# Gates and branch products of the second block: 512 weight columns move instead of 256 token columns

## The reference

```python
z = h @ w_in                              # gz: its last 4 * 1024 columns
branches = (gmlp, pool, sparse_attention, conv)   # four tensors, 256 tokens x 256 features
gates = sigmoid(gz.reshape(B, S, 4, 1024))
y = gates[:, :, 0] * (branches[0] @ w_branch[0])
for n in range(1, 4):
    y = y + gates[:, :, n] * (branches[n] @ w_branch[n])
return y @ w_out
```

## Time and profile before

| | |
|---|---|
| median of three runs | 1937.95 us |
| profiled execution | 1937.7 us |
| its span (first to last instruction) | 1936.0 us |
| PE busy | 1923.7 us, 99% |
| DVE busy | 1380.9 us, 71% |
| ACT busy | 928.1 us, 48% |
| POOL busy | 237.5 us, 12% |

### The profile page before, as it was taken

The page is one execution under the profiler, slowest core; times in us unless marked ns, Lnnn a source line. Parts: engine busy times, 40 slices in busy tenths (PEclk is TensorE's granted clock), DMA queues, the critical chain, the costliest instruction groups (busy, mean ns, idle before and its releaser), DMA issues.

```text
span 1936.0 us, 29945 instructions
## 1 busy us (share of the span) xinstructions
PE 1923.7 (99%) x11950; PEld 1723.8 (89%) x11950; DVE 1380.9 (71%) x1588; ACT 928.1 (48%) x1032; POOL 237.5 (12%) x195
## 2 busy tenths in 40 slices
PE   9999999999999999999999999999999999999998
PEld 7999888889998888888899998888888899998887
DVE  7777766668677666766769677667766769677666
ACT  6564444346545344544554445444544554446443
POOL 0000000000001000000049250000000049250000
PEclk9999999999999999999999999999999999999999
DMA  7544555554356555555444555555555454555553
GB/s 280 193 153 174 176 196 194 184 187 172 131 199 210 190 193 174 193 190 192 163 175 153 175 194 193 183 191 181 202 192 189 167 177 153 173 191 179 188 193 109
DMA packets 50738, 353.37 MB, mean 183 GB/s; under 512 B 6064, under 2 KB 6192, under 8 KB 9040
## 3 DMA queue, kind: packets, MB, share of 16 engines
q1 hardware_dynamic: 47952, 341.93, 50.6%
q0 software_dynamic: 2400, 9.99, 1.5%
q10 hardware_dynamic: 288, 0.05, 0.0%
HBM read 349.85 MB, written 2.10 MB: 182 GB/s over the span
## 4 chain that ended last, share of the span: by engine, by line
PE 90%; DVE 7%; ACT 2%; issue 1%; DMA 0%; DVEq 0%; POOL 0%; POOLq 0%; SPq 0%; ACTq 0%
PE ps L225 21%; PE ps L190 18%; PE ps L191 18%; PE ps L192 18%; PE ps L227 11%; DVE w_lo L166 2%; DVE conv_y L2123 1%; ACT w_hi L159 1%; DVE score L2171 1%; PE ps L1286 1%; ACT a L1667 0%; DVE top L2166 0%; PE ps L2304 0%; DVE score L2143 0%; DVE a L395 0%
## 5 line engine op out<-in xcount | busy, mean ns | idle before, releaser
L166 DVE TENSOR_TENSOR w_lo<-raw,w_hi 128x2048 fp32r<-128x2048 f32 x317 | 734.6, 2321 | 279.8 <-ACT w_hi L159 278.8
L159 ACT ACTIVATE w_hi<-raw 128x2048 fp32r<-128x2048 f32 x317 | 606.3, 1915 | 402.4 <-PE ps L192 226.1
L225 PE MATMUL ps<-a,w_hi 128*128 128x512 f32 x1792 | 449.7, 392 | 2.6 <-DVE w_lo L166 1.4
L225 PEld LDWEIGHTS ps<-a,w_hi 128*128 128x128 f32 x1792 | 325.6, 189 | 67.2 <-DVE a L395 2.8
L190 PE MATMUL ps<-mixH,w_hi 128*128 128x256 f32 x1168 | 334.4, 286 | 0.3
L191 PE MATMUL ps<-mixL,w_hi 128*128 128x256 f32 x1168 | 330.4, 283 | 0.0
L192 PE MATMUL ps<-mixH,w_lo 128*128 128x256 f32 x1168 | 330.3, 283 | 0.0
L190 PE MATMUL ps<-w_hi,mixH 128*128 128x512 f32 x736 | 287.7, 391 | 0.0
L191 PE MATMUL ps<-w_lo,mixH 128*128 128x512 f32 x736 | 287.2, 390 | 0.0
L192 PE MATMUL ps<-w_hi,mixL 128*128 128x512 f32 x736 | 286.4, 389 | 0.0
L227 PEld LDWEIGHTS ps<-a,w_lo 128*128 128x128 f32 x1792 | 244.4, 190 | 17.5
(11 more groups left out here) (382 smaller groups left out, 2035.6 us busy)
## 6 DMA issues: line engine op xcount, KB each, us to landing
raw<-in_w_b SPq DMA_DIRECT2D x198, 1024.0 KB, 5.0
raw<-in_w_a SPq DMA_DIRECT2D x124, 1024.0 KB, 4.8
rows<-in_post_gains POOLq DMA_DIRECT2D x6, 512.0 KB, 4.3
rows<-in_rows_a POOLq DMA_DIRECT2D x2, 1028.0 KB, 7.1
raw<-in_w_a SPq DMA_DIRECT2D x4, 512.0 KB, 6.9
x<-in_x SPq DMA_DIRECT2D x2, 512.0 KB, 5.5
bias_line<-a_gates POOLq DMA_DIRECT2D x1, 1024.0 KB, 4.8
out<-x SPq DMA_DIRECT2D x4, 256.0 KB, 2.0
```

The source lines that it names most:

```text
L159: act.activation(k.w_hi[:, s, :], k.raw[:, s, :], ACT.Copy).then_inc(k.hi_ready, 1)
L166: dve.tensor_tensor(k.w_lo[:, s, :], k.raw[:, s, :], k.w_hi[:, s, :].bitcast(F32), ALU.subtract).then_inc(k.lo_ready, 1)
L225: pe.matmul(both, hi[:, kt, cols], k.a[:, :, kt, :], start=kt == 0, stop=False)
```

## The change

- **Gates**: chunk 9+2g and chunk 10+2g now hold 512 gate columns together, the first with k-tiles 0 to 3, the second with 4 to 7. `gate(i)` calls `t_chunk` with 512 columns: activations stationary, 24 matmuls of 512 weight columns in a chunk. The result lies token by feature in two banks (one for each tile of 128 tokens), banks 6 and 7 for even pairs, 0 and 1 for odd ones, accumulated over two chunks. ACT makes the tanh after every second chunk, two of 512 columns.
- **Branch products**: chunk 25+i holds 512 output columns (half h = i//2) of two branches (q = i%2). It is computed first for token tile 0, then for tile 1, 24 matmuls of 512 columns. DVE multiplies tile 0 by its gates as soon as that half of the chunk is done (`branch_tile`), tile 1 after the chunk.
- **The sum over the branches** of a half of the features is complete only after two chunks. POOL writes it to `mixed[h][tt]`, and in half 1 DVE may overwrite the products only after POOL's last addition of half 0 (`mix_ready`).
- **Transposes**: PE transposes `mixed` back to feature by token, eight transposes for each half (`mixed_transpose`), half 0 between the products 27 and 28, half 1 between the output chunks 29 and 30. ACT and DVE then split the transposed sum out of PSUM.
- Other small tiles move to other PSUM banks, and the weights are packed on the host to match.

```diff
-                for i in range(4):
-                    g = gated[i % 2]
-                    for n in (0, 2):
-                        pool.wait_ge(branch_ready.sem, branch_ready.at(l, NBR * i + n + 2))
-                        pool.tensor_tensor(g[n], g[n], g[n + 1], ALU.add).then_inc(ch.sem, ch.one())
-                    pool.wait_ge(ch.sem, ch.at(l))
-                    pool.tensor_tensor(g[0], g[0], g[2], ALU.add).then_inc(mix_ready.sem, 1)
+                for h in range(2):
+                    for tt in range(TT):
+                        g = gated[tt]
+                        pool.wait_ge(branch_ready.sem, branch_ready.at(l, NBR * 2 * h + 2 * tt + 2))
+                        pool.tensor_tensor(g[0], g[0], g[1], ALU.add).then_inc(ch.sem, ch.one())
+                    for tt in range(TT):
+                        g = gated[tt]
+                        pool.wait_ge(branch_ready.sem, branch_ready.at(l, NBR * (2 * h + 1) + 2 * tt + 2))
+                        pool.tensor_tensor(g[2], g[2], g[3], ALU.add).then_inc(ch.sem, ch.one())
+                        pool.wait_ge(ch.sem, ch.at(l))
+                        pool.tensor_tensor(mixed[h][tt], g[0], g[2], ALU.add).then_inc(mix_ready.sem, 1)
...
                 def gate_in(i):
-                    act.wait_ge(k.chunk_done, st.results(l, G0 + i))
-                    act.activation(flat(gates[:, 2 * i:2 * i + 2, :]), k.ps[:, (i + 1) % 2, :], ACT.Tanh, scale=0.5)\
-                       .then_inc(f_evicted.sem, 1)
+                    if i % 2 == 1:
+                        g = i // 2
+                        for tt in range(TT):
+                            if tt == 0:
+                                act.wait_ge(gate_tile.sem, gate_tile.at(l, g + 1))
+                            else:
+                                act.wait_ge(k.chunk_done, st.results(l, G0 + i))
+                            act.activation(gates_t[:, tt, g // 2, g % 2, :], k.ps[:, (6, 0)[g % 2] + tt, :], ACT.Tanh, scale=0.5)\
+                               .then_inc(gate_evicted.sem, 1)
                     high.upto(G0 + i + 3)
...
-                for i in range(4):
-                    high.upto(min(BR + 3 + i, F0[1] - 1))
-                    act.wait_ge(mix_ready.sem, mix_ready.at(l, i + 1))
-                    act.activation(flat(nH[:, 2 * i:2 * i + 2, :]), gated[i % 2][0], ACT.Copy, scale=0.5)\
-                       .then_inc(mixH_ready.sem, 1)
+                for h in range(2):
+                    high.upto((BR + 4, BR + 6)[h])
+                    for b in range(2):
+                        i = 2 * h + b
+                        act.wait_ge(mixT_done.sem, mixT_done.at(l, i + 1))
+                        act.activation(flat(nH[:, 2 * i:2 * i + 2, :]), k.ps[:, mixed_banks[h][b], :], ACT.Copy, scale=0.5)\
+                           .then_inc(mixH_ready.sem, 1)
...
+                def gate_branches(i):
+                    h, q = i // 2, i % 2
+                    for tt in range(TT):
+                        if tt == 0:
+                            dve.wait_ge(branch_tile.sem, branch_tile.at(l, i + 1))
+                        else:
+                            dve.wait_ge(k.chunk_done, st.results(l, BR + i))
+                        if h == 1:
+                            dve.wait_ge(mix_ready.sem, mix_ready.at(l, tt + 1))
+                        for n in range(2):
+                            dve.scalar_tensor_tensor(gated[tt][2 * q + n], gates_t[:, tt, 2 * q + n, h, :], 1.0,
+                                                     k.ps[:, 4 * ((i + 1) % 2) + 2 * n + tt, :], ALU.add, ALU.mult)\
+                               .then_inc(branch_ready.sem, 1)
+
+                for i in range(3):
                     low.upto(BR + 2 + i)
...
+                    gate_branches(i)
+                mix_low(0)
+                gate_branches(3)
                 low.upto(BR + 6)
-                mix_low(3)
+                mix_low(1)
...
+                def branch(i):
+
+                    s, q = (BR + i) % SLOTS, i % 2
...
+                    pe.wait_ge(k.lo_ready, st.count(l, BR + i))
+                    for tt in range(TT):
+                        for n in range(2):
+                            for kk in (2 * n, 2 * n + 1):
+                                a = [v[:, tt * P:(tt + 1) * P] for v in aop(4 * q + kk)]
+                                ins = product(pe, k.ps[:, 4 * ((i + 1) % 2) + 2 * n + tt, :], a, (hi[:, kk, :], lo[:, kk, :]),
+                                              kk == 2 * n, kk == 2 * n + 1)
+                        ins.then_inc(branch_tile.sem if tt == 0 else k.chunk_done, 1)
+
+                def mixed_transpose(h):
+
+                    pe.wait_ge(mix_ready.sem, mix_ready.at(l, 2 * h + 2))
+                    for b, bank in enumerate(mixed_banks[h]):
+                        for kk in range(2):
+                            for tt in range(TT):
+                                ins = pe.transpose(k.ps[:, bank, kk * SEQ + tt * P:kk * SEQ + (tt + 1) * P],
+                                                   mixed[h][tt][:, (2 * b + kk) * P:(2 * b + kk + 1) * P], k.ident)
+                        ins.then_inc(mixT_done.sem, 1)
...
+                branch(1)
+                pe.wait_ge(branch_ready.sem, branch_ready.at(l, NBR))
+                branch(2)
+                pe.wait_ge(branch_ready.sem, branch_ready.at(l, NBR * 2 + 2))
+                mixed_transpose(0)
+                branch(3)
                 pe.wait_ge(branch_ready.sem, branch_ready.at(l, NBR * 3))
+                pe.wait_ge(mix_split.sem, mix_split.at(l, 2))
...
                     t_chunk(k, pe, WO + i, range(2 * i, 2 * i + 2), DM, nop, t_out, i == 0, False)
+                    if i == 0:
+                        pe.wait_ge(branch_ready.sem, branch_ready.at(l, NBR * 4))
+                        mixed_transpose(1)
```

More of the change, by code:

```diff
@@ L1409, in second_block @@
                  [GU[:, n * 512:(n + 1) * 512] for n in range(3)] + [yb2[:, :, :].rearrange("p t n -> p (t n)")]]
+        gates_t = gates[:, :, :].rearrange("p (t n h a) m -> p t n h (a m)", t=TT, n=NBR, h=2)
         pz = sb("pz", [P, 2, POOL_PAD + SEQ])
@@ L1416, in second_block @@
         conv_y = sb("conv_y", [P, 2, SEQ])
+        mixed = [[qkF[:, 2 * tt:2 * tt + 2, :].rearrange("p f n -> p (f n)") for tt in range(TT)],
+                 [v[:, :, :].rearrange("p f n -> p (f n)") for v in (idxF, conv_y)]]
+        mixed_banks = ((4, 6), (0, 1))
         conv_p = sum4[:, :, 0:SEQ]
@@ L1880, in _ @@
                     half = slice(e * 64, (e + 1) * 64)
-                    ins = act.activation(yH[half, 2 + j, :], k.ps[half, 4 + 2 * e, j * SEQ:(j + 1) * SEQ], ACT.Copy,
+                    ins = act.activation(yH[half, 2 + j, :], k.ps[half, 4 - e, j * SEQ:(j + 1) * SEQ], ACT.Copy,
                                          scale=par[half, PB_PS + j:PB_PS + j + 1])
@@ new lines, in mix_low @@
+                def mix_low(h):
+                    for b in range(2):
+                        i = 2 * h + b
+                        dve.wait_ge(mixH_ready.sem, mixH_ready.at(l, i + 1))
+                        dve.scalar_tensor_tensor(flat(nL[:, 2 * i:2 * i + 2, :]), k.ps[:, mixed_banks[h][b], :], 0.5,
+                                                 flat(nH[:, 2 * i:2 * i + 2, :]).bitcast(F32), ALU.mult, ALU.subtract)\
+                           .then_inc(mix_split.sem, 1)
+                def gate_branches(i):
[11 more added lines that the diff above has]
+                               .then_inc(branch_ready.sem, 1)
@@ L2490, in _, with gate @@
                 feature(6)
+                def gate(i):
+                    g, half = (i - 9) // 2, (i - 9) % 2
+                    pe.wait_ge(k.lo_ready, st.count(l, M0 + i))
+                    if half == 0 and g == 0:
+                        pe.wait_ge(rel_ready.sem, rel_ready.at(l, 1))
+                    elif half == 0 and g == 1:
+                        pe.wait_ge(f_evicted.sem, f_evicted.at(l, 6))
+                    elif half == 0:
+                        pe.wait_ge(gate_evicted.sem, gate_evicted.at(l, 2 * (g - 1)))
+                    t_chunk(k, pe, M0 + i, range(4 * half, 4 * half + 4), 512, nop,
+                            lambda tt, h: k.ps[:, (6, 0)[g % 2] + tt, :], half == 0, half == 1,
+                            tile_done=gate_tile.sem if half == 1 else None)
                 def to_features(bank, src, by=None):
@@ L2515, in _ @@
                 feature(8)
-                feature(9)
+                gate(9)
                 def scores(qt):
@@ L2529, in _ @@
                 scores(1)
-                feature(10)
+                gate(10)
                 pe.wait_ge(rel_ready.sem, rel_ready.at(l, 1))
@@ L2533, in _ @@
                 for i in range(11, 17):
-                    feature(i)
+                    gate(i)
                 pe.wait_ge(exp_ready.sem, exp_ready.at(l, 2))
@@ L2542, in _ @@
                 ins.then_inc(pT_done.sem, 1)
-                feature(17)
```

(17 more changed lines are left out.)

63 lines of the change are left out of this document (20 added, 43 removed).

## The result

The changed kernel takes 1949.70 us (median of four runs, 1949.27 to 1951.04), the kernel before beside it 1937.99 (four runs). The ratio is 1.0061, 95% interval [1.0050, 1.0073]: slower by 11.7 us, where +8.6 to +8.8 was forecast. The profiled execution took 1949.27 with a span of 1947.6 (before 1937.7 and 1936.0), so that profile against profile the difference is 11.6.

The account below looks back on a forecast made before the run. PE, busy 1923.7 of 1936.0 us, was taken as the bound. Per layer -2.4 (gates) -1.2 (products) +2.0 (transposes) +3.1 +2.9 (waits) = +4.4, two layers +8.8: 1946.6 us, 8-in-10 range 1940.5 to 1951.5.

Parts of the forecast that it names:

- PE's rate: Gate and product chunks: 24 matmuls of 512 columns at 0.2275 us instead of 48 at 0.120, saving 0.30 us a chunk.
- The rival of an absent saving: 512-column matmuls run slower in the gates than in output chunks; up to 3.6 us a layer lost, 1953.8 us; chance 0.03.
- Chunks 9 to 16 gain nothing: Top-k stretch: DVE has no gap, so PE's saved 2.4 us become waiting ahead of chunks 15 and 17; taken as 0.
- Chunks 17 to 24: Later gate chunks: DVE has slack again, so eight chunks at 0.30 us count in full, 2.4 us a layer.
- The tight place at chunk 20: Gates: chunk 20's low half follows the DVE row at 1082.72; it could cost 0.5 us.
- The first wait: Ahead of the half 0 transposes, behind chunk 27: PE waits 3.1 us a layer for POOL's sum of tile 1.
- the steps given: Branch products: timed chain of DVE splits, products and POOL additions, with additions beside splits lengthened; tile 1's sum done at 19.5.
- the scale t: Branch products: time in us since the first matmul of chunk 25, used for the forecast's chain of events.
- The second wait: Ahead of the half 1 transposes, behind output chunk 29: PE waits 2.9 us a layer, POOL blocked by low halves 30 and 31.
- Rival 2: Branch products: half 0 waits some 3 us, half 1 not at all; +1.5 us a layer, 1940.9 us; chance 0.11.
- POOL's sums hide: Branch products: sums cost PE almost nothing and the kernel gets faster; -1.5 us a layer, 1934.9 us; chance 0.08.
- a rival with a chance of 0.06: PE's clock falls to 1.2 GHz behind four long waits, half a chunk each, 2.7 us apiece; 1957 us; chance 0.06.

Follow-up runs that it names:

- the last kernel: Changed kernel with transposes in mid-chunk, DVE's new top-k order, and low halves 29 and 31 moved out of the way of POOL's sums: 1928.86 us, 0.9953 of before.
- the kernel with the first wait filled: Changed kernel with twelve matmuls of 512 columns that do no work put on PE ahead of the half 0 transposes: 1949.42 us.
- the one with the top-k order: Changed kernel with DVE re-ordered: low half 15 ahead of the masks, six convolution taps moved behind low half 18: 1945.67 us.
- the kernel with both waits filled: Changed kernel with matmuls that do no work on PE ahead of both groups of transposes (12 for half 0, 11 for half 1): 1946.44 us.

## Why the prediction was right or wrong

- **PE's rate** (0.30 us a chunk): right. The distances are 0.2275, and the last kernel's budget closes with it. (The output chunk that gave the rate, at 1188.34, lies behind the sublayer, in the second feed-forward network and not the first; its shape is the same.) The rival of an absent saving falls.
- **Chunks 9 to 16 gain nothing**: right. Forecast waits 1.4 and 0.9, measured 1.49 and 0.74. Two experiments show that it was DVE's order, and that it can be mended. Missed was that DVE already set the start of chunk 17 before, by about 0.4 us.
- **Chunks 17 to 24** gain 2.4: chunk 25 starts 2.49 earlier. The tight place at chunk 20 cost nothing.
- **The first wait** (3.1 us): measured 3.19, and by the steps given. On the scale t, chunk 25 at 1114.76, low half 28 is done at 11.1 (forecast 10.8), the sum of tile 0 at 17.0 (16.75), of tile 1 at 19.5 (19.5). The split beside the sum is its cause: moved away, the wait is 1.28.
- **The second wait** (2.9 us): measured 2.65, the reason right and a step wrong. POOL was not blocked by both splits in one piece to 33.0: it got its turn between them, and its last sum stood in the second. Rival 2's argument against itself had this sequence. The two ends agree because either way POOL is free only behind the second split; the slower clock of chunk 28 moved both sides by the same.
- **The rivals that POOL's sums hide, or that half 1 does not wait**: fell.
- **What was mis-sized: the clock.** The forecast put the term at zero and left it to a rival with a chance of 0.06, at 2.7 us behind each of four waits. Measured: two falls of about 1.7 us in the profile of the changed kernel, 3.3 us by the kernel without them. 1946.6 and 3.3 are 1949.9, against 1949.7 measured. The rival had the mechanism, with too many falls and too large a price: the clock fell behind two of the four waits ahead of transposes, and the slow stretch is about 3 us with eight matmuls where twelve (half a chunk) were reckoned. No fall came behind the 1.49 and 0.74 us waits in the gates. The Trainium skill's page "TensorE: Matmul & The Clock Gate" (section "HAM oscillation — how this bites in real kernels") describes matmul bursts that restart slow behind waits, in an example with waits of about 3 to 5 us; the trace agrees that matmuls can restart slow, here behind single waits of 2.65 to 3.33 us. Two waits of 3 us a layer deserved more than 0.06.

What stays open: why the clock falls behind one wait and not the next like it. Behind 2.65 us it fell in the kernel with the first wait filled and in the one with the top-k order, and not in the changed kernel, where it had fallen behind the first wait; behind 3.33 us it fell in one layer and not in the other of the same execution. All that the profiles show is that in the sublayer it never fell behind a wait of 1.96 us or less (that one stands in the gates of the second layer of the kernel with both waits filled), and that in the kernels where no wait was longer it fell nowhere in these two layers.

## What to carry to other kernels

A sum that is complete with every chunk hides behind the next one; one that is complete only with the second chunk puts its whole chain on the path, unless the consumer is moved by as much (half a chunk was enough for most of it here). A wait of PE like those here (2.65 to 3.33 us) can cost some 1.6 us more than its length, in slow matmuls behind it, and that part is not in the table of waits: look at the timeline and the granted clock of the few us behind it. And when the bounding engine gets faster, go through the others' order again; where DVE's splits stood in the top-k stretch was worth 4 to 5.5 us here, and 1 in the kernel before.

## What the runs showed of the hardware

- **A DVE split, with two inputs in SBUF, and a POOL addition shut each other out, for the length of one operation.** The additions beside a low-half split took 3.19 to 3.35 us instead of 1.3, and a split that began together with an addition 3.44 instead of 2.29. The gate products on DVE, with one input from PSUM, did not do this: the addition at 1127.13 lay beside two of them, among them the row at 1126.97, and took 1.30. The Trainium skill's page "SBUF — State Buffer" (section "Who interferes with whom") says that a DVE instruction with two SBUF inputs contends with a GpSimd instruction that reads SBUF, and that one with at most one, outside the modes that use two port pairs, does not; the rows agree.
- **Who wins when both begin at once is not fixed.** At 1122.41 in the changed kernel the addition went first (1.30) and the split took 3.44; at 1122.62 in the profile with both waits filled it was the reverse, 2.29 and 3.44, although the two programs are the same up to there in that layer. The sum of half 0 came 0.9 us earlier for it. Both layers of an execution went the same way, and the other six kernels with this change went as the changed one; what decides it stays open.
- **A fall of the clock need not show in the time where one would look.** With the first wait filled the total was the same within 0.3 us, since the fall had moved to the second wait; only the windows told a right theory from a wrong one.
